# A hybrid attention and mLSTM step: the last 40 modulation pieces move from TensorE to VectorE beside the even projection

## The chip, the cores and the metric

The kernel runs on one core of a Trainium2 chip. The metric is the time of one execution in microseconds (us), measured on the device. The core has five engines with a queue of instructions each: PE (matrix products), DVE (VectorE), ACT (ScalarE), POOL (GpSimd) and SP, which here only issues DMAs. They wait for each other with semaphores. All work data lies in SBUF, and PE writes its results to banks of PSUM.

## The reference

One inference step of a backbone with two layers. 128 context tokens and 1024 latent tokens go through the same weights, 1152 rows of width 1024. Every layer changes its normed input and its residual by a modulation that depends only on the conditioning vector; there are two such vectors, one for the context tokens and one for the latent tokens:

```
mod = silu(cond) @ w_mod[li] + b_mod[li]            # (1024) @ (1024, 6144), two conds, two layers
sh1, sc1, g1, sh2, sc2, g2 = split(mod, 6)
h = rms_norm(x, norm1) * (1 + sc1) + sh1
if li % 2 == 0:                                      # layer 0
    p = h @ w_in_even                                # 7 x 512 columns and 16 gate columns
    da_q, da_k, da_v, ml_q, ml_k, ml_v, ml_o, gates = split(p)
    out = concat(diff_attention(rope(norm(da_q)), rope(norm(da_k)), da_v),
                 rms_norm(mlstm_both_directions(ml_q, ml_k, ml_v, gates)) * sigmoid(ml_o)) @ w_out_even
else:                                                # layer 1: grouped-query attention
    out = gqa(h) @ w_out_odd
x = x + g1 * out
h = rms_norm(x, norm2) * (1 + sc2) + sh2
x = x + g2 * (silu(h @ w_gate) * (h @ w_up)) @ w_ffn_out
```

The context tokens read only context tokens; latent tokens read both. All values are float32. The products of the tokens are made with three float32r products each (high by high, low by high, high by low parts).

## The kernel before

Tokens lie in 9 tiles of 128 (`NT`). The stages run one after the other, each a block in which the five engines have their own list of instructions. In the part that matters here they are: the first norm, the even projection (`project`), the gate rows of the mLSTM (`mlstm_gates`), its q/k stage, its scan, its output stage (the last three in `mlstm`); then attention, the output projection, the feed-forward part and the whole odd layer.

**The modulation** of both layers is one long product: two rows (the silu of the two conds) by a weight of 1024 x 12288. It is cut into 48 pieces of 256 columns (1 MB each). `ModulationPieces` does a piece as 8 matmuls with the two rows as the weights and the 256 columns as the moving side (L217), so only two rows of PSUM are used. The profile shows each as two records. ACT copies the two rows out (L240) and, except for the first pieces, issues a DMA that puts them into the scratch `mod_rows` (L244). The first 8 pieces, which the first norm needs, are done in that stage. The other 40 are needed only after the mLSTM and are spread over stages: 12 in `mlstm_gates`, 5 in the q/k stage (two halves of a piece per tile from tile 4 on), 20 in the scan, 3 in the output stage. All of these share one PSUM bank (`mod_row_bank`), so PE starts a piece only after ACT has copied the one before. In the output stage (`mod_rest`) all rows are loaded back, transposed on PE and combined with the bias on DVE.

**The even projection** has 7 chunks of 512 columns by 9 tiles, 24 matmuls per tile into one of three PSUM banks. SP loads a chunk's weights as two units of 1 MB (L502), one chunk ahead; ACT makes the high part of each unit (`high`, L525), POOL the low part (L548), then PE can use the chunk. For chunks 0 and 1 (queries and keys of the attention) DVE evicts (L622), norms and rotates each tile, with POOL's help. For chunks 2 to 6 DVE only evicts. SP stores each tile of 256 KB to the scratch `mixer_in` (L511). ACT's list for a chunk begins with `high` of the next chunk. Chunks 2 to 5 run in a hardware loop of two chunks per turn.

**The gates stage**: PE makes the gate products (54 KB of rows), ACT takes an Exp and a Ln, then DVE computes the gate rows in a long chain; ACT takes the Exp of these rows (L1821), and PE turns them into columns (L1857). ACT copies 7 modulation rows before that Exp and 5 after it.

**The q/k stage** per tile: SP loads q, k, v (L1892 to L1894), POOL scales k (L1905), PE turns q and k and makes the scores (L1917), DVE copies these (L1955). After tile 2's loads SP issues four pieces (L194). **The scan** has 18 turns, one per tile and direction: POOL prepares k and the state, PE turns the row of gates, DVE and ACT make the weights (L2111, L2095), DVE multiplies them by the scores (L2117), PE makes the products (L2076), DVE takes them (L2128 to L2148). In a turn PE does three halves of a piece (turns 0 and 1) or one before the products, and one half after. **The output stage** per tile: ACT squares and takes the sigmoid of the output gate (L2194), POOL multiplies (L2186), DVE applies it (L2229), PE turns the tile.

Of the kernel before, what the change touches and what calls it, by code (L numbers as in the profile page):

```python
# [22 lines left out]
ALU = mybir.AluOpType  # L23
AX = mybir.AxisListType

P = 128
# [11 lines left out]
MOD_PIECES = N_MOD // 256  # L38
MOD_FIRST = 8
MOD_GATES = 12  # L40
# [34 lines left out]
class Program:  # L75
# [55 lines left out]
    def load_parameters(self):  # L131
# [3 lines left out]
        with ExitStack() as s:  # L135
# [3 lines left out]
            with nc.Block() as block:  # L139
# [24 lines left out]
                @block.gpsimd  # L164
                def _(pool):
                    pool.memset(self.minus_half[:], -0.5)
                    pool.memset(self.minus_one[:], -1.0)


    class ModulationPieces:  # L170

        def __init__(self, program, stack, name, slots, first, end, rows, sums=None):
            self.program, self.slots, self.first, self.end, self.rows, self.sums = program, slots, first, end, rows, sums
            self.banks = len(rows)
            self.raw = program.sb(stack, name, [P, slots, 2048])
            self.row = program.sb(stack, name + "_row", [2, 2, 256])
            self.loaded = [program.sem(f"{name}_loaded{i}") for i in range(slots)]  # L180
            self.used, self.row_read = program.sem(name + "_used"), program.sem(name + "_row_read")
            self.turned = program.sem(name + "_turned") if sums is not None else None
            self.stored = [program.sem(f"{name}_stored{i}") for i in range(2)] if sums is None else []
            self.n_loads = first
            self.n_steps = self.n_copies = 0
            self.total = end - first

        def load(self, sync, end):
            w = self.program.t["w_mod"]
            for i in range(self.n_loads, min(end, self.end)):  # L190
                n = i - self.first
                if n >= self.slots:
                    sync.wait_ge(self.used, n - self.slots + 1)
                sync.dma_start(self.raw[:, n % self.slots], w[i // MOD_PIECES, i % MOD_PIECES]).then_inc(self.loaded[n % self.slots], 16)  # L194
            self.n_loads = max(self.n_loads, min(end, self.end))
# [9 lines left out]
        def multiply(self, pe, halves):  # L205

            nc = self.program.nc
            silu = self.program.silu_cond[:].rearrange("p (c k) -> p k c", c=2)
            for _ in range(min(halves, 2 * self.total - self.n_steps)):
                n, half = self.n_steps // 2, self.n_steps % 2  # L210
                slot = n % self.slots
                if half == 0:
                    pe.wait_ge(self.loaded[slot], 16 * (n // self.slots + 1))
                    if n >= self.banks:
                        pe.wait_ge(self.row_read, n - self.banks + 1)
                for k in range(4 * half, 4 * half + 4):
                    mm = nc.tensor.matmul(self.rows[n % self.banks][0:2, 0:256], silu[:, k], self.raw[:, slot, k * 256:(k + 1) * 256],  # L217
                                          start=(k == 0), stop=(k == KB - 1))
                if half == 1:
                    mm.then_inc(self.used, 1)  # L220
                    if self.sums is not None and n > 0:
                        self.turn(pe, n - 1)
                    if self.sums is not None and n == self.total - 1:
                        self.turn(pe, n)
                self.n_steps += 1

        def wait_stored(self, engine):
            for i in range(2):
                engine.wait_ge(self.stored[i], 16 * ((self.total + 1 - i) // 2))

        def copy_rows(self, act, pieces):
            nc = self.program.nc
            for _ in range(min(pieces, self.total - self.n_copies)):
                n = self.n_copies
                act.wait_ge(self.used, n + 1)
                if n >= 2 and self.sums is not None:
                    act.wait_ge(self.turned, n - 1)
                if n >= 2 and self.sums is None:
                    act.wait_ge(self.stored[n % 2], 16 * (n // 2))
                nc.scalar.activation(self.row[:, n % 2], self.rows[n % self.banks][0:2, 0:256], ACT.Copy).then_inc(self.row_read, 1)  # L240
                if self.sums is None:
                    act.wait_ge(self.row_read, n + 1)
                    i = self.first + n
                    nc.scalar.dma_start(self.program.t["mod_rows"][:, 2 * i * P:2 * (i + 1) * P], self.row[:, n % 2]).then_inc(self.stored[n % 2], 16)  # L244
                self.n_copies += 1
# [26 lines left out]
    def norm(self, layer, which, gate_out=None, ahead=None):  # L272
# [15 lines left out]
        with ExitStack() as s:  # L288
# [6 lines left out]
            if first:  # L295
                row_banks = self.ps(s, "mod_row_banks", [P, 2, 512])
                sums = self.ps(s, "mod_sums", [P, 2 * MOD_FIRST, 2])
                pieces = self.ModulationPieces(self, s, "mod_raw", 3, 0, MOD_FIRST, [row_banks[:, 0], row_banks[:, 1]], sums)
            with nc.Block() as block:
# [88 lines left out]
                def _(pe):  # L388
# [5 lines left out]
                    if first:  # L394
                        pieces.multiply(pe, 2 * MOD_FIRST)
# [2021 lines left out]
```

## Time and profile before

| what | us |
|---|---|
| median of three runs | 3937.58 |
| lowest and highest | 3936.36, 3940.97 |
| the profiled execution | 3939.41 |
| its span in the trace | 3937.6 |
| PE busy in the span | 3455.3 (88%) |
| DVE, POOL, ACT busy | 1847.2, 1818.4, 1088.3 |

The trace is one execution. Busy time of an engine is the time in which it executes an instruction; a row of a timeline gives the start, the duration, the engine and line, the tile written and the tiles read, the number of instructions in the row, and in brackets how long the engine had been idle and what ended that. Line numbers are those of the kernel before.

### The profile page before, as it was taken

What the parts mean: (1) busy time and instruction counts of PE and PEld (TensorE: products, weight loads), DVE (VectorE), ACT (ScalarE), POOL (GpSimd) and SP (SyncE); (2) the same over time, 40 slices, a digit from 0 to 9 for tenths busy, and PEclk for the clock granted to TensorE, in tenths of its full rate; (3) what the DMA queues carried; (4) which work ended last, traced back from release to release, by engine and by line L of the source; (5) the groups of instructions that cost most, each with busy time, mean ns of one, the idle gap of its engine ahead of it and who ended that gap; (6) DMA issues with size and microseconds to landing.
All of it is one profiled execution on the core that took longest, in us unless ns stands there. A gap on an engine that the chain in (4) does not pass through costs nothing. (4 is left out here: it accounts for less than half of the span.)

```text
span 3937.6 us, 52363 instructions
## 1 busy us (share of the span) xinstructions
PE 3455.3 (88%) x17872; PEld 2950.9 (75%) x17872; DVE 1847.2 (47%) x3389; ACT 1088.3 (28%) x2474; POOL 1818.4 (46%) x1700
## 2 busy tenths in 40 slices
PE   5999879757769899999997886888889799999999
PEld 3778645446657799999997664777767699999998
DVE  3731234577753333333333676888873333333333
ACT  4100011246641301101101215888870301101110
POOL 0621014435541265455453355888860246446445
PEclk9999989969989899999998896999999899999999
DMA  4122254320020101101101212000001110110111
GB/s 186 57 98 89 91 202 170 105 86 15 15 82 22 54 33 53 43 32 53 43 32 49 81 48 71 17 16 16 16 12 80 55 42 32 53 43 32 53 43 48
DMA packets 119336, 233.04 MB, mean 59 GB/s; under 512 B 64160, under 2 KB 71696, under 8 KB 109072
## 3 DMA queue, kind: packets, MB, share of 16 engines
q1 hardware_dynamic: 119056, 231.41, 16.9%
q8 instruction: 69, 1.13, 0.1%
q14 instruction: 51, 0.42, 0.0%
q10 hardware_dynamic: 160, 0.08, 0.0%
HBM read 197.82 MB, written 34.43 MB: 59 GB/s over the span
## 5 line engine op out<-in xcount | busy, mean ns | idle before, releaser
L784 POOL TENSOR_TENSOR x<-x,ff_gated 128x512 f32<-128x512 f32 x396 | 512.2, 1294 | 319.8 <-DVE ff_gated L869 296.5
L778 POOL TENSOR_TENSOR ff_lo<-ff_raw,ff_hi 128x1024 fp32r<-128x1024 f32 x132 | 328.7, 2498 | 547.0 <-ACT ff_hi L745 547.0
L869 DVE TENSOR_TENSOR ff_gated<-ff_y_banks,gate_tokens 128x512 f32<-128x512 f32 x396 | 273.9, 692 | 412.3 <-PE ff_y_banks L843 412.3
L582 PE MATMUL tile_sum<-w_hi,tokens_hi 128*128 128x512 f32 x1008 | 404.4, 401 | 70.5 <-DVE w_lo L613 46.0
L745 ACT ACTIVATE ff_hi<-ff_raw 128x1024 fp32r<-128x1024 f32 x132 | 137.9, 1060 | 1118.3 <-PE ff_y_banks L843 720.5
L858 DVE TENSOR_TENSOR ff_silu<-ff_silu,ff_up_banks 128x384 f32<-128x384 f32 x132 | 72.5, 550 | 717.9 <-PE ff_up_banks L814 717.9
L583 PE MATMUL tile_sum<-w_lo,tokens_hi 128*128 128x512 f32 x1008 | 402.1, 399 | 0.0
L584 PE MATMUL tile_sum<-w_hi,tokens_lo 128*128 128x512 f32 x1008 | 401.3, 398 | 0.0
L810 PE MATMUL ff_gate_banks<-tokens_hi,ff_hi 128*128 128x384 f32 x1056 | 354.4, 336 | 19.4 <-POOL ff_lo L778 19.4
L811 PE MATMUL ff_gate_banks<-tokens_lo,ff_hi 128*128 128x384 f32 x1056 | 353.9, 335 | 0.0
L811 PE MATMUL ff_up_banks<-tokens_lo,ff_hi 128*128 128x384 f32 x1056 | 353.2, 334 | 0.0
L810 PE MATMUL ff_up_banks<-tokens_hi,ff_hi 128*128 128x384 f32 x1056 | 352.9, 334 | 0.0
L841 PE MATMUL ff_y_banks<-ff_hi,ff_hidden_hi 128*128 128x512 f32 x792 | 310.2, 392 | 9.1 <-DVE ff_hidden_lo L862 9.1
L842 PE MATMUL ff_y_banks<-ff_lo,ff_hidden_hi 128*128 128x512 f32 x792 | 310.0, 391 | 0.0
L843 PE MATMUL ff_y_banks<-ff_hi,ff_hidden_lo 128*128 128x512 f32 x792 | 310.0, 391 | 0.0
L582 PEld LDWEIGHTS tile_sum<-w_hi,tokens_hi 128*128 128x128 f32 x1008 | 194.3, 193 | 117.7 <-DVE w_lo L613 48.3
L1481 POOL TENSOR_TENSOR probs<-probs,row_total 128x1152 f32<-128x1152 f32 (+1 forms) x144 | 276.1, 1917 | 11.3
L1680 DVE TENSOR_REDUCE chunk_minima<-score_banks 128x1 f32<-128x384 f32 (+1 forms) x400 | 211.3, 541 | 66.7 <-PE score_banks L1522 64.7
L548 POOL TENSOR_TENSOR w_lo<-w_raw,w_hi 128x2048 fp32r<-128x2048 f32 x20 | 91.8, 4609 | 326.3 <-ACT w_hi L525 326.3
L814 PE MATMUL ff_gate_banks<-tokens_hi,ff_lo 128*128 128x384 f32 x1056 | 240.5, 335 | 0.0
L1617 ACT ACTIVATE probs<-score_banks,minus_max 128x384 f32<-128x384 f32 (+1 forms) x400 | 224.8, 575 | 55.7 <-PE turn_banks L1539 31.3
L814 PE MATMUL ff_up_banks<-tokens_hi,ff_lo 128*128 128x384 f32 x1056 | 239.6, 334 | 0.0
(256 smaller groups left out, 7361.8 us busy)
## 6 DMA issues: line engine op xcount, KB each, us to landing
ff_raw<-in_w_ffn SPq DMA_DIRECT2D x132, 512.0 KB, 3.2
mod_raw_scan<-in_w_mod SPq DMA_DIRECT2D x28, 1024.0 KB, 4.9
scratch_mixer_in<-tile_out SPq DMA_DIRECT2D x90, 256.0 KB, 2.0
w_raw<-in_w_in_even SPq DMA_DIRECT2D x14, 1024.0 KB, 6.2
mod_raw_gates<-in_w_mod SPq DMA_DIRECT2D x12, 1024.0 KB, 4.9
q_double<-scratch_mixer_in SPq DMA_DIRECT2D x72, 128.0 KB, 2.3
mod_raw<-in_w_mod SPq DMA_DIRECT2D x8, 1024.0 KB, 4.8
w_raw<-in_w_in_odd SPq DMA_DIRECT2D x6, 1024.0 KB, 6.0
```

Of the source, the lines that this page charges most:

```text
L582: nc.tensor.matmul(acc, self.hi[k // 4][:, k % 4, mine], w_hi, start=(k == 0), stop=False)
L583: nc.tensor.matmul(acc, self.hi[k // 4][:, k % 4, mine], w_lo, start=False, stop=False)
L584: mm = nc.tensor.matmul(acc, self.lo[k // 4][:, k % 4, mine], w_hi, start=False, stop=(k == KB - 1))
L778: pool.tensor_tensor(lo[:, u], raw[:, slot], hi[:, u].bitcast(F32), ALU.subtract).then_inc(lo_done, 1)
L784: pool.tensor_tensor(self.x[:, t, cols], self.x[:, t, cols], y[:, m % YB], ALU.add).then_inc(added, 1)
L810: nc.tensor.matmul(acc[:, n, 0:TC], wh, self.hi[k // 4][:, k % 4, cols], start=(k == 0), stop=False)
L811: nc.tensor.matmul(acc[:, n, 0:TC], wh, self.lo[k // 4][:, k % 4, cols], start=False, stop=False)
L814: mm = nc.tensor.matmul(acc[:, n, 0:TC], wl, self.hi[k // 4][:, k % 4, cols], start=False, stop=(k == KB - 1))
L841: nc.tensor.matmul(ybank[:, half], hid_hi[:, b, mine], hi[:, 4 + b, cols], start=(b == 0), stop=False)
L842: nc.tensor.matmul(ybank[:, half], hid_hi[:, b, mine], lo[:, 4 + b, cols], start=False, stop=False)
L843: mm = nc.tensor.matmul(ybank[:, half], hid_lo[:, b, mine], hi[:, 4 + b, cols], start=False, stop=(b == 1))
L1481: pool.tensor_tensor(mine, mine, sum_.broadcast_to([P, x.blocks * P]), ALU.mult).then_inc(scaled, 1)
```

## The change

The first 8 pieces stay as they are, but the weight is now laid out in 24 units of 512 columns (2 MB, [128][8][512]), so a piece of 256 columns is loaded in runs of 1 KB. For the other 40 pieces (20 units):

- Beside chunks 2 to 6 of the even projection, four units per chunk, SP loads each unit in four parts of 512 KB (four slots). DVE multiplies each block of 128 x 512 by the silu value of its partition and adds it to a sum (16 operations per unit: 8 blocks for 2 conds; each waits for the operation two before). The sums (128 x 1024 per unit) are stored to a new scratch, `mod_acc`.
- ACT evicts the tiles of these chunks. It does `high` of the next chunk ahead of tile 2's eviction. The loop over chunks is written out. SP's list per tile is: the tile's store, the loads due, the store of a finished sum. At the end of chunk 1 it issues four parts ahead of the weights of chunk 3. At the end of the stage SP waits for the sums' stores.
- In the gates stage SP loads the 20 sums (eight slots), and PE adds the 128 partitions: two matmuls over 512 columns, with weights of 128 x 2 that hold a column of ones for one cond. Two PSUM banks take the rows; ACT copies and stores them, 14 units ahead of the Exp of the gate rows and 6 after it.
- The q/k stage, the scan and the output stage lose their pieces, and the load of `mod_rest` moves from tile 4 to tile 0, its turn from tile 6 to tile 0.

```diff
+    class ModulationSums:
+        UNITS, PARTS, SLOTS = 4, 4, 4
...
+        def load(self, sync, end):
+            w = self.program.t["w_mod"]
+            for n in range(self.n_loads, min(end, self.total * self.PARTS)):
+                if n >= self.SLOTS:
+                    sync.wait_ge(self.added, 4 * (n - self.SLOTS + 1))
+                part = slice(n % self.PARTS * 1024, n % self.PARTS * 1024 + 1024)
+                sync.dma_start(self.raw[:, n % self.SLOTS].rearrange("p k n -> p (k n)"),
+                               w[MOD_FIRST // 2 + n // self.PARTS][:, part]).then_inc(self.loaded[n % self.SLOTS], 16)
...
+        def store(self, sync, end):
+            for n in range(self.n_stores, end):
+                sync.wait_ge(self.added, 2 * KB * (n + 1))
+                sync.dma_start(self.program.t["mod_acc"][n], self.acc[:, n % 2].rearrange("p c n -> p (c n)")).then_inc(self.stored[n % 2], 16)
...
+        def add(self, dve, n):
+            if n >= 2:
+                dve.wait_ge(self.stored[n % 2], 16 * (n // 2))
+            for k in range(KB):
+                part = n * self.PARTS + k // 2
+                if k % 2 == 0:
+                    dve.wait_ge(self.loaded[part % self.SLOTS], 16 * (part // self.SLOTS + 1))
+                for i in range(2):
+                    acc, w, scale = self.acc[:, n % 2, i], self.raw[:, part % self.SLOTS, k % 2], silu[:, i, k:k + 1]
+                    if k == 0:
+                        op = nc.vector.tensor_scalar(acc, w, scale, None, ALU.mult)
+                    else:
+                        dve.wait_ge(self.added, 2 * KB * n + 2 * k + i - 1)
+                        op = nc.vector.scalar_tensor_tensor(out=acc, in0=w, scalar=scale, in1=acc, op0=ALU.mult, op1=ALU.add)
+                    op.then_inc(self.added, 1)
...
# project, SP, after each tile's store
+                                if sums is not None and c >= len(normed):
+                                    parts = sums.UNITS * sums.PARTS
+                                    at = (c - len(normed)) * parts + parts * (t + 1) // NT
+                                    sums.load(sync, at + sums.SLOTS)
+                                    sums.store(sync, at // sums.PARTS)
+                            if sums is not None and c == len(normed) - 1:
+                                sums.load(sync, sums.SLOTS)
...
# project, ACT
+                        if sums is not None and c >= len(normed):
+                            for t in range(NT):
+                                if t == 2 and not (fixed and c == chunks - 1):
+                                    high(c + 1, 1 - parity, True)
+                                act.wait_ge(tile_done, c * NT + t + 1)
+                                act.wait_ge(stored[t], 16 * c)
+                                nc.scalar.activation(ob[:, t], bank[:, t % 3], ACT.Copy).then_inc(tile_read, 1)
+                            return
...
# mlstm_gates, PE
-                    pieces.multiply(pe, 2 * MOD_GATES)
+                    for n in range(units):
+                        pe.wait_ge(acc_loaded[n % SLOTS], 16 * (n // SLOTS + 1))
+                        if n >= 2:
+                            pe.wait_ge(row_read, n - 1)
+                        for i in range(2):
+                            mm = nc.tensor.matmul(row_banks[0:2, n % 2], self.pick[:, i], acc[:, n % SLOTS, i], start=(i == 0), stop=(i == 1))
+                        mm.then_inc(acc_used, 1)
...
# scan, PE
-                        pieces.multiply(pe, 3 if n < 2 else 1)
...
-                        pieces.multiply(pe, 1)
```

## Rows read from the trace of the kernel before

**Rows 1.** Windows at stage borders: busy of five engines, granted PE clock, DMA share, GB/s.

```profile
86.00:457.20 371.20, 356.46 (x1512) 288.49 (x1512) 124.61 (x215) 34.15 (x30) 114.97 (x48) 0.98 0.21 79
457.20:540.70 83.50, 64.17 (x318) 34.32 (x318) 32.56 (x46) 14.25 (x18) 7.86 (x4) 0.90 0.43 158
540.70:601.00 60.30, 40.70 (x224) 27.68 (x224) 12.45 (x18) 7.25 (x14) 17.49 (x11) 0.77 0.74 260
601.00:751.00 150.00, 139.32 (x808) 82.27 (x808) 90.81 (x160) 30.51 (x93) 69.76 (x88) 0.97 0.40 147
751.00:805.00 54.00, 22.30 (x86) 10.36 (x86) 25.56 (x50) 17.38 (x31) 21.68 (x18) 0.71 0.14 46
```

**Rows 2.** Timeline of the projection: weights of chunk 3, last tile.

```profile
218.29 0.99 SPq L502 DMA_DIRECT2D w_raw<-in_w_in_even  x2
...
227.81 1.92 ACT L525 ACTIVATE w_hi<-w_raw 128x2048 fp32r<-128x2048 f32 x1 [1.77 <-DMA w_raw<-in_w_in_even]
...
454.05 0.69 DVE L622 COPY tile_out<-tile_sum 128x512 f32<-128x512 f32 x1 [4.85 <-PE tile_sum L584]
```

**Rows 3.** Timeline of DVE: three forms of operation, each followed by the next start.

```profile
918.21 1.41 DVE L1314 SCALAR_TENSOR_TENSOR first_map<-second_map,row_total,first_map 128x1152 f32<-128x1152 f32 x1
919.54 1.48 DVE L1298 TENSOR_REDUCE chunk_minima<-score_banks 128x1 f32<-128x384 f32 x3
...
64.94 0.69 DVE L366 TENSOR_TENSOR tokens_lo<-h_scaled,tokens_hi 128x512 fp32r<-128x512 f32 x1
65.54 0.42 DVE L364 CAST tokens_hi<-h_scaled 128x512 fp32r<-128x512 f32 x1
```

**Rows 4.** Timeline of POOL and DVE: two places where both read SBUF.

```profile
1196.89 4.60 POOL L548 TENSOR_TENSOR w_lo<-w_raw,w_hi 128x2048 fp32r<-128x2048 f32 x1 [6.91 <-ACT w_hi L525]
...
1199.83 2.22 DVE L681 TENSOR_TENSOR x<-x,tile_out 128x512 f32<-128x512 f32 x1
...
115.09 1.49 POOL L556 TENSOR_TENSOR tile_out<-tile_out,params 128x512 f32<-128x512 f32 x1
...
115.35 1.52 DVE L654 TENSOR_TENSOR tile_out<-rotary_second 128x256 f32<-128x256 f32 x1
```

**Rows 5.** DMA issues of the page: count, KB each, us to landing.

```profile
ff_raw<-in_w_ffn SPq DMA_DIRECT2D x132, 512.0 KB, 3.2
```

**Rows 6.** Timeline of the gates stage: two pieces, the Exp, the column turns.

```profile
486.39 5.40 PE L217 MATMUL mod_row_bank<-mod_raw_gates,silu_cond 128*2 128x256 f32 x16 [5.68 <-ACT mod_raw_gates_row L240]
492.34 3.61 PE L217 MATMUL mod_row_bank<-mod_raw_gates,silu_cond 128*2 128x256 f32 x16 [0.56 <-ACT mod_raw_gates_row L240]
...
514.62 4.04 ACT L1821 ACTIVATE gate_rows<-gate_rows 36x4608 f32<-36x4608 f32 x1
...
535.12 4.98 PE L1857 MATMUL col_bank<-params,gate_rows 36*128 36x36 f32 x54
```

**Rows 7.** Timeline of POOL in the q/k stage: scales of tiles 1, 2, 3.

```profile
547.83 1.49 POOL L1905 TENSOR_SCALAR ml_k<-ml_k 128x512 f32<-128x512 f32 x1 [1.85 <-DMA ml_k<-scratch_mixer_in]
551.51 1.49 POOL L1905 TENSOR_SCALAR ml_k<-ml_k 128x512 f32<-128x512 f32 x1 [2.20 <-DMA ml_k<-scratch_mixer_in]
566.31 1.49 POOL L1905 TENSOR_SCALAR ml_k<-ml_k 128x512 f32<-128x512 f32 x1 [13.31 <-DMA ml_k<-scratch_mixer_in]
```

**Rows 8.** Waits of DVE in the scan: us in total, times, longest.

```profile
DVE ml_weighted L2117 <- ACT ml_weights L2095: 24.2, 18, 1.3
...
DVE ml_num L2128 <- PE ml_num_banks L2076: 8.9, 2, 4.5
DVE ml_inter L2130 <- PE ml_num_banks L2076: 4.0, 2, 2.8
```

**Rows 9.** Timeline of DVE in the output stage: gate products of tiles 0, 4, 8.

```profile
759.13 0.69 DVE L2229 TENSOR_TENSOR ml_h<-ml_h,ml_gate 128x512 f32<-128x512 f32 x1 [4.78 <-POOL ml_gate L2186]
...
788.33 0.69 DVE L2229 TENSOR_TENSOR ml_h<-ml_h,ml_gate 128x512 f32<-128x512 f32 x1
...
799.16 0.69 DVE L2229 TENSOR_TENSOR ml_h<-ml_h,ml_gate 128x512 f32<-128x512 f32 x1
```

More of the change, by code:

```diff
@@ L167, in _, with __init__ @@
                     pool.memset(self.minus_one[:], -1.0)
+                    for i in range(2):
+                        for j in range(2):
+                            pool.memset(self.pick[:, i, j:j + 1], float(i == j))
     class ModulationPieces:
[L175 to L178, printed above, removed]
+        def __init__(self, program, stack, name, slots, total):
+            self.program, self.slots, self.total = program, slots, total
+            self.raw = program.sb(stack, name, [P, slots, KB, 256])
@@ L184, in __init__, with load @@
[L184 to L191, printed above, removed]
+            self.used, self.row_read, self.turned = (program.sem(f"{name}_{x}") for x in ("used", "row_read", "turned"))
+        def load(self, sync):
+            for n in range(self.total):
                 if n >= self.slots:
@@ L203, in turn, with multiply @@
             mm.then_inc(self.turned, 1)
-        def multiply(self, pe, halves):
+        def multiply(self, pe):
             nc = self.program.nc
             silu = self.program.silu_cond[:].rearrange("p (c k) -> p k c", c=2)
[L209 to L225, printed above, removed]
@@ L227, in wait_stored @@
-        def wait_stored(self, engine):
+            for n in range(self.total):
+                pe.wait_ge(self.loaded[n % self.slots], 16 * (n // self.slots + 1))
+                if n >= 2:
+                    pe.wait_ge(self.row_read, n - 1)
+                for k in range(KB):
+                    mm = nc.tensor.matmul(self.banks[0:2, n % 2, 0:256], silu[:, k], self.raw[:, n % self.slots, k], start=(k == 0), stop=(k == KB - 1))
+                mm.then_inc(self.used, 1)
+                if n > 0:
+                    self.turn(pe, n - 1)
@@ L228, in wait_stored @@
             for i in range(2):
-                engine.wait_ge(self.stored[i], 16 * ((self.total + 1 - i) // 2))
-        def copy_rows(self, act, pieces):
+                sync.wait_ge(self.stored[i], 16 * (self.total // 2))
+        def add(self, dve, n):
             nc = self.program.nc
[L233 to L245, printed above, removed]
+            silu = self.program.silu_cond[:].rearrange("p (c k) -> p c k", c=2)
+            if n >= 2:
+                dve.wait_ge(self.stored[n % 2], 16 * (n // 2))
+            for k in range(KB):
+                part = n * self.PARTS + k // 2
[9 more added lines that the diff above has]
+                    op.then_inc(self.added, 1)
@@ L304, in _ @@
                             sync.dma_start(x[:, t], self.t["x"][:, t]).then_inc(loaded[t], 16)
-                        pieces.load(sync, MOD_FIRST)
+                        pieces.load(sync)
                     if ahead is not None:
@@ L394, in _ @@
                     if first:
-                        pieces.multiply(pe, 2 * MOD_FIRST)
+                        pieces.multiply(pe)
                     for n, (t0, cnt, k) in enumerate(items):
@@ L437, in _, with project @@
                         nc.vector.tensor_copy(out[:, n // 2, 512:1024], bank[:, n]).then_inc(read_odd, 1)
-    def project(self, weights, chunks, out=None, residual=None, normed=(), ahead=None):
+    def project(self, weights, chunks, out=None, residual=None, normed=(), ahead=None, modulation=False):
         nc = self.nc
@@ L456, in over_chunks @@
         def over_chunks(eng, body):
+            if modulation:
+                for c in range(chunks):
+                    body(c, c % 2, c >= 2)
+                return
             body(0, 0, False)
@@ L480, in project @@
             bank = self.ps(s, "tile_sum", [P, 3, 512])
+            sums = self.ModulationSums(self, s, chunks, len(normed), work) if modulation else None
             with nc.Block() as block:
@@ L667, in body @@
                                     rotary(c, t - 2)
+                            return
+                        if sums is not None:
+                            for u in range(sums.UNITS):
+                                sums.add(dve, (c - len(normed)) * sums.UNITS + u)
                             return
@@ L1754, in mlstm_gates @@
             cb = self.ps(s, "col_bank", [P, 2, 512])
-            pieces = self.ModulationPieces(self, s, "mod_raw_gates", 4, MOD_FIRST, MOD_FIRST + MOD_GATES, [self.mod_row_bank])
+            SLOTS = 8
+            units = 2 * MOD_UNITS - MOD_FIRST // 2
+            acc = self.sb(s, "mod_acc_back", [P, SLOTS, 2, 512])
+            rows = self.sb(s, "mod_rows", [2, 2, 512])
+            row_banks = self.ps(s, "mod_row_banks", [P, 2, 512])
+            acc_loaded = [self.sem(f"mg_acc_loaded{i}") for i in range(SLOTS)]
+            row_stored = [self.sem(f"mg_row_stored{i}") for i in range(2)]
+            acc_used, row_read = self.sem("mg_acc_used"), self.sem("mg_row_read")
             with nc.Block() as block:
@@ L1931, in _ @@
                             scores(t - 1)
-                        if t > 3:
-                            pieces.multiply(pe, 2)
                     scores(NT - 1)
@@ L2001, in _ @@
                     sync.dma_start(CT[:], self.t["state"]).then_inc(state_in, 16)
-                    pieces.load(sync, A1)
                 @block.gpsimd
```

101 lines of the change are left out of this document (60 added, 41 removed).

## The prediction

> **What bounds the kernel now.** I read the busy shares first, then one table of windows cut at the stage borders, then the waits of the scan, and last single instructions on the timeline. The change lies in the first 805 us of a span of 3937.6; the rest only reads its result. In the windows [rows 1] the reader is to see that the stages have different limits. The even projection (86 to 457) is PE's: 356 of 371 us busy, DVE at 125, ACT at 34, the DMA engines at a share of 0.21. In the gates stage PE is busy 64 of 83.5, though its own job there is small. In the q/k stage DMA is at 0.74 and PE at 41 of 60. The scan has PE at 139 of 150. The output stage has no engine above half.
>
> In the projection PE stands 371.2 - 356.5 = 14.7 us in all [rows 1]. Near its end a tile takes DVE's wait plus its copy, 4.85 + 0.69 = 5.54 us [rows 2]; the stage ends at about 457.3.
>
> **The projection: DVE gets 320 operations.** DVE loses the evictions of chunks 2 to 6 (45 of 0.69) and gains 20 units of 16 operations over 512 columns: 280 that multiply, add and read two SBUF operands, and 40 that only multiply. The trace has the first form at 1152 columns: start to next start 1.33 us [rows 3]. Its neighbour, a plain two-operand subtraction over 512, repeats after 0.60 and lasts 0.69 [rows 3]. By columns alone 1.33 makes 0.59 at 512, so 0.60 is the lower bound; nothing overlapped gives the full 0.69; and if the wait on the operation two before leaves a gap in place of the overlap of 0.08 to 0.09 that these rows have, of 0.05 say, 0.74, the upper bound. I take 0.66, between 0.60 and 0.69 and nearer to the second for that wait. The 40 multiplies read one operand, as the cast does at 0.42 [rows 3]. So 280 x 0.66 + 40 x 0.42 = 202.
>
> To this comes POOL. Beside a 4.60 us subtraction for the low weights on POOL, a DVE addition of two SBUF operands lasted 2.22 instead of 0.69 and ended when POOL did; beside a POOL multiply of 1.49 a DVE addition took 1.52 [rows 4]. POOL started there although DVE's operations followed each other without a gap. So each low half costs DVE its 4.60: two halves for each of chunks 3 to 6 are 36.8 us. DVE's work is then 239. It starts when the first part is in: SP reaches the loads at about 218.3 [rows 2], a 512 KB load lands after 3.2 [rows 5], so 221.5, and ends at 460.5; the last 512 KB store makes it 464. That is **+7** on 457. With 0.60 DVE would end at 444 and PE bind instead; with 0.74 at 483, +29.
>
> The Trainium skill, "SBUF — State Buffer", section "Who interferes with whom", says that DVE with two SBUF inputs and a reading POOL exclude each other whole, and that issue order decides who waits. These rows agree for DVE's side; that POOL can be the one kept out is the third rival below.
>
> PE's side: DVE evicts late where chunks 1 and 2 begin, behind its norms and rotations; at chunk 2 ACT now does, which saves half of the 14.7 at most, 7. But ACT does the high halves of chunk 3 before it evicts tile 2, and SP puts four parts (2 MB) ahead of that chunk's weights. The second high half began at 227.8 before [rows 2]; with 2 MB more at 512 KB per 2 to 3.2 us it begins near 233 and tile 2 goes at 235. PE, with three banks, stands from about 223: some 12 us, against 7 saved. PE ends near 462, so this hides under DVE's 464. In later chunks the weights' loads are queued on SP behind parts that wait for DVE; by the pace above tile 2 is evicted 24 to 27 us into a 50 us chunk, and PE needs its bank at 28: no stall, a small margin. If DVE had slack, PE alone would give +2 to +6. Loads: 80 parts are 40 MB; at the q/k stage's 260 GB/s [rows 1] 161 us, hidden; one at a time, 80 x 3.2 = 256, another 17 on the end.
>
> **Gates stage.** A piece of 256 columns cost 3.61 on PE in 16 records and 0.56 waiting for ACT to empty the one bank [rows 6]; twelve of them fill the stage. Now 20 units of two matmuls over 512 columns: half a piece's columns, so 1.8 each, with two banks, so without the wait. From 486.4, 14 units end near 512; the Exp that began at 514.6 and took 4.04 [rows 6] begins near 513 and ends at 517. PE has gone two units further meanwhile; four more end at 524.1, and the 4.98 of column turns [rows 6] at 529.1 instead of 540.1: **-11**. The DVE chain of gate rows is not changed and is done by then. The 20 loads of 512 KB fit (2 to 3.2 us each from 457 on, eight slots). Bounds: -13 with the Exp earlier; if every unit ran at half clock, 1.8 more each, +24.
>
> **q/k stage.** Four 1 MB loads go out amid the tiles' loads, and POOL's scale of tile 3 comes at 566.3 after 13.31 us without its k [rows 7]. Two halves of a piece per tile follow on PE. Without both, tiles run at the distance from tile 1 to tile 2, about 3.7: tile 3 at 555.2, tile 8 at 573.6, then scale, the POOL memset and the last scores, to about 579.5 instead of 601: **-21** (17 to 24, as a tile takes 4.2 or 3.3).
>
> **Scan.** DVE waits 8.9 in two waits for the products that PE does behind three halves of a piece in turns 0 and 1, and 4.0 in two waits elsewhere [rows 8]. In the other turns it waits for ACT's weights, 24.2 over 18 [rows 8], which no piece feeds. So 8.9 and a part of 4.0: **-10.5**, from -8 to -12.9. The steady turns stay as they are although PE loses most of its load.
>
> **Output stage.** The gate product comes at 759.1 and, three pieces later, at 788.3 for the fifth tile; then every 2.71 (10.83 for four) [rows 9]. ACT's row copies stand in front of the sigmoids in its queue. Free of them the fifth comes 10.9 after the first, instead of 29.2: **-18.3**, from -14 (the parameter load, now at tile 0, holding a tile) to -19.
>
> **At nothing:** the first eight pieces, now in 1 KB runs: hidden while PE's 3.61 per piece [rows 6] covers the landing of 1 MB. One at a time at 6.4 (two of 512 KB) they would cost 8 x 2.8 = 22; three slots overlap them, so 0 to 2. The four memsets stand ahead of idle time on POOL.
>
> **Sum:** -11 - 21 - 10.5 - 18.3 = -61, +7, is -54. The profiled execution took 3939.4, 1.8 above the median of the runs; against the median the forecast is 3937.6 - 54 = 3884.
>
> **The rivals.**
> *A: DVE binds the projection outright.* At 0.74, or with loads one at a time, the projection grows by 17 to 29: 3937.6 - 61 + 29 = 3906. For: each operation waits on the one two before. Against: the multiply-add at 1152 columns [rows 3] has no more overhead than the subtraction.
>
> *B: PE's clock.* Where PE is lightly loaded the granted clock is low: 0.71 in the output stage and 0.77 in the q/k stage against 0.97 in the scan, where pieces fill PE [rows 1]. With the pieces gone the gates stage may lose the full clock for half its units, 10 x 1.8 = 18: 3902. Against: there the units run back to back, and the scan's and q/k stage's limits are ACT, POOL and DMA. The Trainium skill, "TensorE: Matmul & The Clock Gate", section "HAM oscillation — how this bites in real kernels", says that a PE with gaps falls back to half clock again and again. The rows agree; it would give this rival.
>
> *C, slower than before: POOL is kept out.* If DVE's unbroken two-operand chain holds the shared way, the low halves wait. They are ready some 36 us into a chunk (the high halves at 24 to 27, two times 4.60 after) and needed at 50, so a delay under 14 is free. Were they kept out until DVE's four units are through, which with DVE's lag of 15 is at 65, and then took 9.2, PE would stand about 25 at each of four chunk starts: +100 and no +7, so 3937.6 - 61 + 100 = 3977. It decides from 61/4, 15 us of standing, on. Against it: POOL's multiply that got in between two adjacent DVE operations [rows 4].
>
> *D: DVE keeps up.* At 0.60 PE ends the projection, with +2: 3879.
>
> **How the numbers follow.** Forecast 0.58, A 0.14, B 0.09, C 0.08, D 0.08, and 0.03 for a mixture that lands near before. The forecast's own range is 3870 to 3898; with A, B and D, 3862 to 3912, the lower end by the stages' far bounds together (-13 - 24 - 12.9 - 19 with +0 is -69, and some 6 more). A measurement of this kernel can tell about 0.2%, 7.9 us. Slower: C, 0.08, and 0.01 of A at a far worse price; same: 0.03; faster: 0.88.
>
> **What would show it.** Right: DVE nearly unbroken from 221 to 460 with operations 0.66 apart and jumps of 4.6 at the low halves; PE standing once, at chunk 2's fifth or sixth tile; the column turns ending 11 earlier against the stage's start; POOL's k scales about 3.7 apart; no wait for the products over 1 in turns 0 and 1; gate products 2.7 apart from the first. Wrong: PE waiting for low or high halves at chunk starts, DVE waiting for parts, or units 3.5 apart in the gates stage.

## The result, and the profile after

The changed kernel takes 3892.8 us in the median of four runs (3885.0 to 3893.8), the kernel before 3938.8 (3936.4 to 3941.0): ratio 0.9879, 95% interval 0.9862 to 0.9896. That is 46 us less; 54 had been forecast. The profiled execution took 3892.9, its span is 3891.1.

A stage is measured from the first instruction that belongs to it to the first of the next one (PE's first product of the projection, POOL's first fill of the gates and q/k stages, POOL's first column copy of the scan, SP's first load of the output stage and of the attention).

| stage | before | after | difference | forecast |
|---|---|---|---|---|
| to the projection | 86.2 | 87.0 | +0.8 | 0 to 2 |
| even projection | 371.1 | 382.0 | +10.9 | +7 |
| gates | 83.4 | 76.6 | -6.8 | -11 |
| q/k | 60.4 | 38.3 | -22.1 | -21 |
| scan | 149.8 | 136.9 | -13.0 | -10.5 |
| output | 55.9 | 37.4 | -18.5 | -18.3 |
| the rest, not changed | 3130.8 | 3132.9 | +2.1 | 0 |

The rest took between 3126.1 and 3135.4 in the fourteen profiled executions of this study, without any edit to it. So a single time is not worth more than some 5 us, and the experiments below are read by their stages.

First the windows of the changed kernel at these borders, to be set beside [rows 1]: busy time of PE, its weight loads, DVE, ACT and POOL, the granted PE clock, DMA share and GB/s.

```profile
87.00:469.00 382.00, 356.29 (x1512) 287.37 (x1512) 321.98 (x489) 59.53 (x75) 117.40 (x49) 0.97 0.60 214
469.00:545.60 76.60, 58.87 (x206) 26.20 (x206) 32.57 (x46) 21.51 (x26) 7.84 (x3) 0.83 0.41 145
545.60:584.00 38.40, 22.37 (x144) 20.44 (x144) 12.46 (x18) 5.38 (x9) 17.57 (x12) 0.78 0.61 185
584.00:720.80 136.80, 84.46 (x488) 78.32 (x488) 86.71 (x160) 23.01 (x72) 69.76 (x88) 0.78 0.02 8
720.80:758.20 37.40, 10.31 (x38) 6.87 (x38) 26.19 (x50) 16.22 (x28) 22.86 (x18) 0.50 0.22 66
```

DVE went from 125 to 322 us of the projection, while PE's busy time there is what it was. In the scan PE fell from 139 to 84 and its granted clock from 0.97 to 0.78, and yet the stage got shorter.

The costs on DVE, as groups of the projection: busy time, mean duration, idle time before them.

```profile
L272 DVE SCALAR_TENSOR_TENSOR qk_work<-mod_unit,silu_cond,qk_work 128x512 f32<-128x512 f32 x280 | 187.2, 743 | 0.0
L269 DVE TENSOR_SCALAR qk_work<-mod_unit,silu_cond 128x512 f32<-128x512 f32 x40 | 44.1, 1143 | 18.2 <-DMA mod_unit<-in_w_mod 18.2
```

187.2 / 280 is 0.669 per multiply-add: the 0.66 that was taken between [rows 3]'s 0.60 and 0.69. The 40 multiplies should have cost 0.42 each, 17; they hold 44.1, and DVE waited 18.2 for parts, in five waits (4.7 of it before the first part, 13.5 inside the stage). Both belong to one picture, POOL's low halves (the low parts of a chunk's two weight units) and DVE on the timeline at two of the four places:

```profile
231.88 11.04 POOL L596 TENSOR_TENSOR w_lo<-w_raw,w_hi 128x2048 fp32r<-128x2048 f32 x2 [17.06 <-ACT w_hi L565]
284.67 9.36 POOL L596 TENSOR_TENSOR w_lo<-w_raw,w_hi 128x2048 fp32r<-128x2048 f32 x2 [41.76 <-ACT w_hi L565]
```

```profile
234.74 8.46 DVE L269 TENSOR_SCALAR qk_work<-mod_unit,silu_cond 128x512 f32<-128x512 f32 x2 [0.99 <-DMA mod_unit<-in_w_mod]
...
287.12 7.20 DVE L269 TENSOR_SCALAR qk_work<-mod_unit,silu_cond 128x512 f32<-128x512 f32 x2 [4.43 <-DMA mod_unit<-in_w_mod]
```

Each pair of low halves runs where DVE pauses for a part: 284.67 lies in DVE's idle time of 4.43 before 287.12. The pair asked for at 231.88 got in only when DVE stopped near 233.75, hence 11.04 instead of 9.36. When the part comes, DVE's two multiplies stand until POOL is done (7.20 instead of 0.87). They read one SBUF operand each, so what stands beside POOL here is not one of the two-operand additions. The four pairs (here and at 335.2 and 386.2) show this alike. The parts are late there because SP has just put 2 MB of weights in front of them, the same weights whose high halves POOL was waiting for:

```profile
273.49 1.86 SPq L533 DMA_DIRECT2D w_raw<-in_w_in_even  x2
...
276.35 0.45 SPq L243 DMA_DIRECT2D mod_unit<-in_w_mod  x1
```

DVE ends at 465.5, the last store and the border follow at 469.0. PE stood long only once, 11.1 at chunk 2, and was done at 462:

```profile
PE tile_sum L630 <- ACT tile_out L575: 12.8, 4, 11.1
```

```profile
456.17 9.37 DVE L272 SCALAR_TENSOR_TENSOR qk_work<-mod_unit,silu_cond,qk_work 128x512 f32<-128x512 f32 x14
```

In the gates stage ACT and PE, where [rows 6] show 514.62 and 535.12 before (57.4 and 77.9 after the stage's start; here 57.7 and 71.0):

```profile
526.67 4.04 ACT L1890 ACTIVATE gate_rows<-gate_rows 36x4608 f32<-36x4608 f32 x1
```

```profile
531.34 8.72 PE L1929 MATMUL mod_row_banks<-mod_acc_back,pick_row 128*2 128x512 f32 x16 [3.44 <-ACT mod_rows L1876]
539.99 5.04 PE L1936 MATMUL col_bank<-params,gate_rows 36*128 36x36 f32 x54
```

Four units (16 records) remain behind the Exp. PE stood 3.44, nearly all of it beside the Exp, which ends at 530.71, and then needs 8.72 for them. ACT also waited for its two row buffers to be stored:

```profile
ACT mod_rows L1876 <- DMA scratch_mod_rows<-mod_rows: 8.1, 6, 2.2
```

The other stages, first POOL's scales of tiles 1 to 3 in the q/k stage [rows 7], then DVE's waits in the scan [rows 8], then gate products of tiles 0, 1 and 4 of the output stage [rows 9]:

```profile
552.85 1.49 POOL L1977 TENSOR_SCALAR ml_k<-ml_k 128x512 f32<-128x512 f32 x1 [2.27 <-DMA ml_k<-scratch_mixer_in]
556.34 1.49 POOL L1977 TENSOR_SCALAR ml_k<-ml_k 128x512 f32<-128x512 f32 x1 [2.00 <-DMA ml_k<-scratch_mixer_in]
559.79 1.49 POOL L1977 TENSOR_SCALAR ml_k<-ml_k 128x512 f32<-128x512 f32 x1 [1.96 <-DMA ml_k<-scratch_mixer_in]
```

```profile
DVE ml_weighted L2181 <- ACT ml_weights L2160: 24.2, 18, 1.3
DVE ml_arg L2175 <- PE ml_r_bank L2122: 22.0, 17, 9.2
...
DVE ml_inter L2194 <- PE ml_num_banks L2142: 0.2, 1, 0.2
```

```profile
729.04 0.69 DVE L2290 TENSOR_TENSOR ml_h<-ml_h,ml_gate 128x512 f32<-128x512 f32 x1 [4.78 <-POOL ml_gate L2249]
731.80 0.69 DVE L2290 TENSOR_TENSOR ml_h<-ml_h,ml_gate 128x512 f32<-128x512 f32 x1
...
739.99 0.69 DVE L2290 TENSOR_TENSOR ml_h<-ml_h,ml_gate 128x512 f32<-128x512 f32 x1
```

The distance of these tiles is 3.5 (between 2.7 and 4.4 among the last four), the scan's waits for the products went from 8.9 and 4.0 to nothing and 0.2, and gate products follow every 2.7 from the first.

### The profile page after: what moved, and what is told of

Same layout as the page of the kernel before. It is cut to its first block and busy times, and to the rows that moved or that the text cites. A ratio compares the mean times of both kernels' runs of the same rounds, so it can differ in the third digit from the quotient of the medians.

```text
span 3891.1 us, 51407 instructions
## 1 busy us (share of the span) xinstructions
PE 3370.2 (87%) x17312; PEld 2930.7 (75%) x17312; DVE 2036.8 (52%) x3664; ACT 1111.2 (29%) x2499; POOL 1825.4 (47%) x1704
## 5 line engine op out<-in xcount | busy, mean ns | idle before, releaser
L1533 POOL TENSOR_TENSOR probs<-probs,row_total 128x1152 f32<-128x1152 f32 (+1 forms) x144 | 276.3, 1919 | 11.3
```

The costliest lines, as they stand in the source:

```text
L1533: pool.tensor_tensor(mine, mine, sum_.broadcast_to([P, x.blocks * P]), ALU.mult).then_inc(scaled, 1)
```

## The experiments

Two questions were open: what sets the end of the projection (DVE's work, the parts' loads, or PE), and why the gates stage gave back 6.8 and not 11. All kernels are the changed kernel with the edit shown.

**e1: no sums at all.**

```diff
-                                sums.add(dve, (c - len(normed)) * sums.UNITS + u)
+                                pass
...
-            units = 2 * MOD_UNITS - MOD_FIRST // 2
+            units = 0
```

> Leaves out the 20 units: no parts are loaded, nothing is added on DVE, nothing stored, and PE adds no partitions in the gates stage (the 40 pieces of the modulation are filled with other numbers). ACT still evicts with the high halves ahead of tile 2. Theory 'adds' (DVE's own work of about 241 us from 223.6 to 465.2 sets the end of the projection): the projection, 382.0 in the changed kernel, falls to about 370, PE standing some 7 us at chunk 2 since the weights of chunk 3 no longer stand behind four parts; the gates stage falls from 76.6 to about 66, the chain of gate rows and columns alone; the run takes about 3870. Theory 'PE' (the order on ACT and SP costs PE the 11 us by which the stage grew): the projection stays near 377 or more.

This kernel leaves out the last 40 pieces (their rows are filled with other numbers). Projection 370.8, gates 65.7, run 3870.0. So with ACT evicting and nothing added the projection is as before (371.1): what PE saved at chunk 2 it lost again to the high halves there (5.6 of standing, in e1). The sums, with their loads and stores, cost 11.2 in the projection, and the units 10.9 in the gates stage.

**e2: the weights' loads earlier, so that they do not stand before the parts.**

```diff
-                        if not last:
+                        if not last and not (modulation and c >= 2):
...
+                                if modulation and 1 <= c < chunks - 2 and t in (5, 7):
+                                    h = (t - 5) // 2
+                                    sync.wait_ge(lo_done, c * 2 + h + 1)
+                                    sync.dma_start(raw[:, h], weights[c + 2, h]).then_inc(raw_loaded[h], 16)
```

> SP issues each chunk's two weight units of 1 MB after tiles 5 and 7 of the chunk two before it, as soon as the low half that used the buffer is done, and no longer both at the start of the chunk before. Theory 'loads' (DVE's 13.5 us of waiting for parts behind 2 MB of weights set the end): those waits go, DVE ends near 452 and the projection takes about 368 to 370. Theory 'adds': the waits go, but they lie where POOL makes the low halves and keeps DVE standing anyway, so DVE stands 9.4 beside POOL in each of four chunks instead of 27 in all, ends 1 to 5 earlier at 460 to 464, and the projection takes 377 to 381. In both PE no longer stands 11 at chunk 2 and ends near 450.

Projection 383.4: neither. DVE's waits for parts inside the stage fell only from 13.5 to about 8, and something new appeared. The low halves of chunks 5 and 6 on POOL, and the DVE rows in which they got in:

```profile
317.06 4.61 POOL L600 TENSOR_TENSOR w_lo<-w_raw,w_hi 128x2048 fp32r<-128x2048 f32 x1 [35.85 <-ACT w_hi L569]
327.10 38.30 POOL L600 TENSOR_TENSOR w_lo<-w_raw,w_hi 128x2048 fp32r<-128x2048 f32 x1 [5.43 <-ACT w_hi L569]
379.01 35.78 POOL L600 TENSOR_TENSOR w_lo<-w_raw,w_hi 128x2048 fp32r<-128x2048 f32 x2 [13.61 <-ACT w_hi L569]
```

```profile
363.41 2.67 DVE L269 TENSOR_SCALAR qk_work<-mod_unit,silu_cond 128x512 f32<-128x512 f32 x2 [2.37 <-DMA mod_unit<-in_w_mod]
...
405.76 9.32 DVE L269 TENSOR_SCALAR qk_work<-mod_unit,silu_cond 128x512 f32<-128x512 f32 x2 [0.20 <-DMA mod_unit<-in_w_mod]
```

The low half asked for at 327.10 was kept out while DVE's chain ran and got in at DVE's pause from 361.04 (363.41 less 2.37); 4.4 later it was done. The pair of 379.01 got in at a pause of 0.20 before 405.76. PE stood for the first of them:

```profile
PE tile_sum L634 <- POOL w_lo L600: 9.3, 1, 9.3
```

This is rival C, on a kernel whose DVE pauses less.

**e3: POOL fills the low halves with zeros.**

```diff
+                            if modulation and c >= 3:
+                                pool.memset(lo[:, parity, h].bitcast(F32), 0.0).then_inc(lo_done, 1)
+                                continue
```

> For chunks 3 to 6 POOL fills the low half with zeros, which reads no SBUF, instead of subtracting (the low products of these chunks are then left out). Theory 'adds, with POOL holding them up': DVE operations beside POOL are no longer long, the 40 first multiplies fall from 1.14 to about 0.45 each, DVE ends some 27 earlier, near 438, and the stage then ends with PE's last tile and its store near 465: 377. Rival 'loads': DVE's operations shorten but it waits for parts as much longer, DVE's end stays near 465 and the projection at 382.

This leaves out the low products of chunks 3 to 6. Projection 376.4. The multiplies fell from 44.1 to 24.1, so it is POOL's subtraction that held them:

```profile
L269 DVE TENSOR_SCALAR qk_work<-mod_unit,silu_cond 128x512 f32<-128x512 f32 x40 | 24.1, 642 | 23.1 <-DMA mod_unit<-in_w_mod 22.3 <-DMA scratch_mod_acc<-qk_work 0.7
```

Both theories had a part: DVE's waits for parts grew from 18.2 to some 30 (7.6 of them within units), since SP hands parts out by PE's tiles, and DVE ended with PE, near 459.

**e4: DVE makes the low halves itself.**

```diff
+                                if u == 1 and c < chunks - 1:
+                                    for h in range(2):
+                                        dve.wait_ge(hi_done, (c + 1) * 2 + h + 1)
+                                        nc.vector.tensor_tensor(lo[:, 1 - parity, h], raw[:, h], hi[:, 1 - parity, h].bitcast(F32),
+                                                                ALU.subtract).then_inc(lo_done, 1)
```

> DVE itself makes the two low halves of chunks 3 to 6, after the second unit of each chunk, at 2.2 us each (the first chunk's halves on DVE take 4.50 for two). Theory 'adds': 8 x 2.2 = 18 replaces 27 of standing beside POOL and part of what parts hide, so DVE ends 5 to 15 earlier, at 450 to 460; the projection then ends with PE, near 378, unless PE stands for the later low halves. Theory 'loads': DVE's end stays at 465 or goes up by 18, and so does the stage, 382 to 400.

Projection 377.6. The groups on DVE show the exchange, 17.9 of subtractions for 26.6 of standing multiplies (44.1 less 17.5):

```profile
L723 DVE TENSOR_TENSOR w_lo<-w_raw,w_hi 128x2048 fp32r<-128x2048 f32 x8 | 17.9, 2282 | 0.0
L269 DVE TENSOR_SCALAR qk_work<-mod_unit,silu_cond 128x512 f32<-128x512 f32 x40 | 17.5, 479 | 20.2 <-DMA mod_unit<-in_w_mod 20.2
```

PE and DVE end this stage together, at 461, PE after the same stand at chunk 2 (11.3).

**e7: e2, and DVE waits for the low halves after its second unit.**

```diff
+                                if u == 1 and c < chunks - 1:
+                                    dve.wait_ge(lo_done, 2 * c + 2)
```

> As e2 (weights early), and DVE waits after the second unit of each chunk 2 to 5 until both low halves of the next chunk are made. Theory 'kept out' (POOL's low half can start only where DVE's unbroken chain of two-operand additions pauses: in e2 one took 38.3 us and PE stood 9.3 for it): each low half gets in at DVE's wait or before it, at 4.6 once it is in and none over about 25 with its waiting; PE does not stand for low halves any more and ends near 452. DVE pays some 9.2 in each of the four chunks, so the projection stays at 378 to 384. Rival 'slow POOL' (the low halves are slowed by the denser loads of e2): they stay long although DVE waits, and DVE's wait grows to 20 or more a chunk, the projection to 400 and more.

Projection 381.9, PE never stood for a low half, and all took 4.5 to 5.2. That fits, but decides little: here all of them got in before DVE's wait. The first did so beside the rotations of chunk 1, the second as DVE's first multiply began, and six between two additions of the running chain, which held DVE up by 4.4 each (the additions took 213.4 in all, against 187.2). So POOL can get in between, as [rows 4] had shown, and in e2 at other times it did not.

**e8: e2 with POOL's fills.**

```diff
+                            if modulation and c >= 3:
+                                pool.memset(lo[:, parity, h].bitcast(F32), 0.0).then_inc(lo_done, 1)
+                                continue
```

> As e2, but POOL fills the low halves of chunks 3 to 6 with zeros (their low products are left out), which reads no SBUF. Theory 'kept out by the read': the fills take 1.8 each although DVE hardly pauses, PE never stands for a low half, DVE has 204 us of work and ends with the parts of the last tiles; PE ends near 450 and the projection takes 366 to 369. Rival 'any POOL instruction is kept out': fills of 10 us and more where DVE's chain is unbroken, PE stands as in e2, 375 or more.

Projection 364.6: fills of 1.8 to 2.0, no stand for a low half, DVE and PE done together near 446.7. A row with two of the fills:

```profile
310.43 3.84 POOL L601 MEMSET w_lo<- 128x2048 f32 x2 [39.66 <-ACT w_hi L569]
```

With POOL filling, the early weights save 11.8 us (376.4 in e3); with POOL subtracting they saved nothing (383.4 in e2, 382.0). So they do help when POOL doesn't read beside DVE's chain.

**e11: the kernel of e2 once more.**

> The kernel of e2 once more, with times. Theory 'kept out by chance': of the eight low halves others are the long ones this time, or none; the executions differ by 5 us and more, and the profiled projection lies anywhere from 372 to 390. Rival 'fixed order': the same two low halves (the second of chunk 5, the pair of chunk 6) are long again, at 38 and 36 us, and the projection takes 383.

Four executions took 3897.0 to 3909.5, and e2 had taken 3891.9: ratio to before 0.9906 (0.9891 to 0.9921), slower than the changed kernel in the median by 9. This time seven low halves took 4.5 to 5.1, those that had been long in e2 for chunk 5 among them, and the last one 58.59. POOL, DVE's next pause, and PE:

```profile
377.33 58.59 POOL L600 TENSOR_TENSOR w_lo<-w_raw,w_hi 128x2048 fp32r<-128x2048 f32 x1 [5.26 <-ACT w_hi L569]
```

```profile
445.86 0.88 DVE L269 TENSOR_SCALAR qk_work<-mod_unit,silu_cond 128x512 f32<-128x512 f32 x2 [14.29 <-DMA mod_unit<-in_w_mod]
```

```profile
PE tile_sum L634 <- POOL w_lo L600: 29.5, 1, 29.5
```

DVE's chain ran to 431.57 (445.86 less 14.29), and POOL ended 4.35 later; PE stood 29.5 and the projection took 403.0, more than the 372 to 390 that had been expected. The same program keeps out other low halves in another execution; what decides which, these runs do not show.

**e10: e2 with fewer pauses** (two parts more ahead of each tile, the first parts after tile 6 of chunk 1, the weights of chunk 3 after tiles 2 and 3).

```diff
-                                    sums.load(sync, at + sums.SLOTS)
+                                    sums.load(sync, at + sums.SLOTS + 2)
```

> As e2 (POOL subtracts), with the weights of chunk 3 after tiles 2 and 3 of chunk 1, the first parts after tile 6 of chunk 1 and two parts more ahead of each tile: DVE hardly pauses. Theory 'kept out by chance': a low half that does not get between two of DVE's operations waits for DVE's next pause; with fewer pauses one or more of the eight low halves lasts over 25 us, PE stands 10 or more for it, and the projection takes 380 to 400 although all loads are earlier. Rival 'the lock only costs DVE its 4.6 each': every low half takes 4.6 to 5.3, DVE ends near 458, PE near 449, the projection takes 371 to 375.

A miss: 409.5, but not by low halves, of which none took over 13.5. With more parts ahead SP stood in its list before the sums' stores, and DVE, with two sums, waited for these: 39.7 in 16 waits. So DVE paused more, and POOL got in. It tells nothing on the chance of being kept out.

**e5: the gates stage alone.** ACT copies two rows ahead of the first Exp and 17 instead of 14 ahead of the second; four row buffers and three banks.

```diff
-        FIRST_ROWS = 14
+        EARLY_ROWS, FIRST_ROWS, ROWS, BANKS = 2, 17, 4, 3
...
+                    take_rows(0, EARLY_ROWS)
                     act.wait_ge(own, self.n_abs)
...
-                    take_rows(0, FIRST_ROWS)
+                    take_rows(EARLY_ROWS, FIRST_ROWS)
```

> Gates stage alone: ACT copies 2 rows ahead of the first Exp and 15 after the Ln, so 17 ahead of the second Exp and 3 after it; four buffers for the rows' stores and three banks on PE. Theory 'rows late' (the 6.8 gained instead of 11 is the six units left after the Exp, done partly at half clock, and waits for two row buffers): the second Exp begins at the end of the DVE chain, 55 to 56 after the stage's start, the columns end by 66 to 68 instead of 76.6, and the run takes about 3884. Rival 'chain': the later end of the chain of gate rows (54.4 after the start instead of 52.3) and a colder PE are all of it; the stage stays over 73.

Gates 64.9, as little as in e1 without any unit (65.7). The Exp of the rows begins 54.5 after the stage's start, and the three rows that are left follow it on ACT while PE turns columns:

```profile
523.56 4.04 ACT L1891 ACTIVATE gate_rows<-gate_rows 36x4608 f32<-36x4608 f32 x1
527.51 0.57 ACT L1876 ACTIVATE mod_rows<-mod_row_banks 2x512 f32<-2x512 f32 x1
```

The run took 3872.5, 12 less than expected; 7 of that lies in the rest, which no edit touched.

**e6, e9, e12: a version from the findings.** e6 joins e2, e4, e5 and the first parts after tile 6 of chunk 1. e9 adds the weights of chunk 3 after tiles 2 and 3 and the two parts more per tile of e10; e12 leaves these two parts out again.

```diff
-                                if modulation and 1 <= c < chunks - 2 and t in (5, 7):
-                                    h = (t - 5) // 2
+                                if modulation and 1 <= c < chunks - 2 and t in ((2, 3) if c == 1 else (5, 7)):
+                                    h = int(t in (3, 7))
```

> A version built from the findings: weights early (e2), the first four parts issued after tile 6 of chunk 1, low halves of chunks 3 to 6 on DVE (e4), rows early (e5). If POOL was what held DVE, and DVE held POOL: DVE has 204 + 18 us of work and ends with the last parts, PE ends near 450 without standing at chunk 2 or for low halves; projection 366 to 369, gates 66 to 68, the rest as in the changed kernel: 3866 to 3870, ratio to the kernel before about 0.982. If DVE's low halves come too late for PE: 375 or more for the projection.

> As e6, with the weights of chunk 3 issued after tiles 2 and 3 of chunk 1 (in e6 the second high half began at 225.7 and PE stood 3.1 for it, with a cold clock behind it) and with SP putting two parts more ahead of each tile, so that DVE waits less for parts. Theory: in e6 PE and DVE end together near 452; now PE ends some 4 to 5 earlier and DVE too, the projection takes 364 to 366 instead of 369.4, the run 3858 to 3862, ratio about 0.980. Rival: DVE's low halves or its sums end later than PE in any case, and the projection stays at 369.

> As e6, with the weights of chunk 3 issued after tiles 2 and 3 of chunk 1, and without the two parts more per tile of e9 (there SP waited on DVE in front of the sums' stores, and DVE then waited 21.3 for these stores). In e9 PE did not stand once after chunk 1 and evicted its last tile at 444.4. Theory: now PE's pace sets the parts' pace too, DVE ends some 447, the store lands by 451, the projection takes 364 to 366 instead of 369.4 in e6, the run 3858 to 3863, ratio about 0.980. Rival: DVE waits for stores or parts all the same and the projection stays over 368.

| kernel | median of five, us | ratio to before (95%) | projection | gates |
|---|---|---|---|---|
| e6 | 3864.4 | 0.9809 (0.9795 to 0.9822) | 369.4 | 64.4 |
| e9 | 3873.6 | 0.9836 (0.9823 to 0.9850) | 380.1 | 65.3 |
| e12 | 3858.2 | 0.9796 (0.9783 to 0.9809) | 364.2 | 64.6 |

e9 is a miss of the same kind as e10: PE was done by 445, but DVE waited for the stores of its sums, so the last store landed at 466:

```profile
DVE qk_work L269 <- DMA scratch_mod_acc<-qk_work: 21.3, 15, 4.5
```

e12 differs from e9 in these two parts alone, and DVE no longer waits for a store. In e12 PE doesn't stand once after chunk 1, PE and DVE end together near 446.5, and the projection is shorter than before the change although DVE does all the sums beside it. Its window of the projection:

```profile
87.20:451.50 364.30, 353.81 (x1512) 286.72 (x1512) 312.67 (x498) 60.06 (x75) 78.36 (x41) 0.98 0.65 224
```

## Why the prediction came out as it did

**Projection, +7 forecast, +10.9 measured.** The sum was near and its parts held: 0.669 per multiply-add, PE's stand of 11.1 at chunk 2 (12 forecast), PE done at 462 (462), DVE as the end (464 forecast with its store, 469.0 measured). DVE began 2 later than worked out, and the stage 1 later. The step "POOL started there although DVE's operations followed each other without a gap. So each low half costs DVE its 4.60" did not describe what happened: POOL went in where DVE paused for parts, which cost 26.6 of standing and 13.5 of waiting, together 40 for the 36.8 of the sum. That the two figures are near is luck: the waits for parts stood at nothing in the sum ("40 MB ... 161 us, hidden") and are one of the prediction's own signs of being wrong. Standing and waiting fell together by the list of SP: parts come late exactly when new weights come. Where POOL did get in between two additions, in e7, the price was about the forecast one, 4.4. e2 and e11 show what happens when the pauses are shorter. In [rows 4] the addition ended 0.56 after POOL, and not with it; that changes no term.

**Rival C** got 0.08 as an outcome and did not come, but its mechanism is real. In e2 and e11 a reading POOL was kept out for 34, 27 and 54 us by DVE's chain, in 4 low halves of 16 counting the one that queued behind another; PE stood 9.3 and 29.5 for it. The argument against it, that POOL's multiply got in between two adjacent operations, is a case that holds at some times and not at others (e7 and e11).

**Gates, -11 forecast, -6.8 measured.** Of the size, not the mechanism: the step "four more end at 524.1". The Exp began 57.7 after the stage's start instead of 55.7, with ACT waiting 8.1 for row stores and its first row only after the Ln; and the four units behind the Exp began 0.6 after its end and took 8.72, not 7.2: 2.0, 0.6 and 1.5 are the 4.2 that are missing, but for 0.1. e5 removes these and brings 11.8 more.

**q/k, scan, output.** -22.1, -13.0 and -18.5 against -21, -10.5 and -18.3. In the scan all of the 8.9 and 4.0 went (0.2 is left), not a part of the 4.0: the far end of that range. That these 12.7 are nearly the whole -13.0 is partly luck: DVE's waits for PE's turn of the gates rose by 3.9 (18.1 to 22.0), although PE had less to do, and its 18 multiplies by the scores took 3.8 less (23.7 to 19.8). No experiment asked why.

**The rest.** The 2.1 more there are within what other executions show. With it the terms are -46.5.

**Rival B** was right on the clock and wrong on its price: granted 0.83 in the gates stage (0.90 before), 0.78 in the scan (0.97), 0.50 in the output stage (0.71). The scan and the output stage became shorter all the same. In the gates stage the four units behind the Exp took 8.72 at a granted 0.81, 1.5 more than forecast, of the 18 that the rival had put there. **Rival A** came half true, with DVE as the end, at 0.669 and not 0.74. **D** did not occur.

## What to carry to other kernels

Work moved to an idle engine is priced also by what that engine shares, not by its idle time alone: in these kernels DVE's chain beside a reading POOL either stood for POOL or kept POOL out, and moving POOL's small job onto DVE itself was cheaper than both (377.6 in e4 against 382.0; with early weights 369.4 in e6, which also loads its first parts earlier, against 383.4 and 403.0 in e2 and e11). Where a late transfer makes an engine pause, look who uses the pause before removing it. When partial results are put in front of a stage's last big step, count how many are left behind that step, and keep stores that another engine waits for out of the way of loads in one list of DMAs (e9, e10).

## What the runs showed of the hardware

A POOL subtraction of 128 x 2048 that took 4.6 alone took 38.3 (e2) and 58.6 (e11) while DVE ran its chain, almost all of it additions with two SBUF operands, 0.67 apart; it ended 4.4 after DVE's next pause, and a pause of 0.20 was enough. In other places of the same chain it got in between two additions at once (4.6 to 5.2 in e7, six of eight). A fill on POOL, which reads nothing, took 1.8 to 2.0 in the same place; in e3 it cost DVE's multiplies 6.6 (24.1 against the 17.5 of e4), where the subtraction had cost 26.6. The Trainium skill, "SBUF — State Buffer", section "Summary: rules for kernel authors", says that the second to issue is blocked until the first finishes. These runs agree that one of the two stands whole. But in e11 POOL stayed blocked while DVE began 85 instructions (54 us at 0.67), so the end of the first did not free it, and having waited longer did not give it the turn.
